# A hybrid encoder trunk: weight granules halved in the attention heads, and the first mixer reordered

## The reference

```
proj = rmsnorm(h, norm_mix) @ w_in[layer]
gate_b, gate_c, u, c_q, c_kv_full, gate_logits = split(proj)
y_a = (gate_b * shortconv(gate_c * u)) @ w_conv_out
# 16 heads, 64 + 32 (rotary) wide; queries and keys come from the latents c_q, c_kv
p = softmax(q k^T * scale + chunk mask);  y_b = (p v) @ w_o
g_a, g_b = sigmoid(gate_logits + b_gate)
h = h + (g_a * y_a + g_b * y_b) @ w_mix_out
```

## Time and profile before

| | before |
|---|---|
| time, median of 3 runs | 1182.83 us (1182.29 to 1185.14) |
| the profiled execution's own time | 1182.17 us |
| its span in the trace | 1180.4 us |
| TensorE busy | 1149.3 us (97%) |
| VectorE / ScalarE / GpSimd busy | 873.6 / 754.4 / 20.0 us |
| mean granted TensorE clock | 0.995 |

### The profile page before, as it was taken

How to read it: one execution, slowest core, us unless ns; L and a number is a source line. 1 busy time by engine, 2 the same in 40 slices (tenths; PEclk the granted TensorE clock), 3 DMA queues, 4 the chain that set the end, 5 groups by cost and what they waited for, 6 DMA issues and landing times.

```text
span 1180.4 us, 15901 instructions
## 1 busy us (share of the span) xinstructions
PE 1149.3 (97%) x5664; PEld 968.5 (82%) x5664; DVE 873.6 (74%) x987; ACT 754.4 (64%) x927; POOL 20.0 (2%) x59
## 2 busy tenths in 40 slices
PE   8999999999999999999999999999999999999986
PEld 7788788888888888887788888888888888888864
DVE  5557667666444546477666779999999999999993
ACT  6546565545444346456566456799878887888882
POOL 3000000000000001000000000000000000000000
PEclk9999999999999999999999999999999999999998
DMA  8755422659556354646333647999999999999991
GB/s 307 246 167 179 154 88 73 215 187 318 181 184 204 107 179 144 200 143 192 137 99 113 204 170 278 386 401 407 396 408 364 408 392 406 364 402 388 401 366 39
DMA packets 120555, 294.98 MB, mean 250 GB/s; under 512 B 9006, under 2 KB 33676, under 8 KB 119964
## 3 DMA queue, kind: packets, MB, share of 16 engines
q1 hardware_dynamic: 119376, 288.66, 67.9%
q0 software_dynamic: 960, 5.28, 1.2%
q10 hardware_dynamic: 140, 0.04, 0.0%
HBM read 292.90 MB, written 1.05 MB: 249 GB/s over the span
## 4 chain that ended last, share of the span: by engine, by line
PE 50%; issue 42%; ACT 4%; DVE 2%; DMA 1%; POOL 0%; SPq 0%; POOLq 0%; DVEq 0%; ACTq 0%
PE bank L1518 15%; PE bank L1519 15%; PE bank L1520 15%; PE bank L1556 2%; ACT w_hi L647 1%; DMA raw<-in_w_in 1%; PE bank L1719 1%; PE bank L1699 1%; ACT p_buf L775 1%; DVE mixed L1215 1%; PE bank L1707 1%; PE bank L1691 1%; DVE small L1218 1%; ACT pT L781 1%; PE bank L1755 0%
## 5 line engine op out<-in xcount | busy, mean ns | idle before, releaser
L1014 DVE TENSOR_TENSOR w_lo<-raw,w_hi 128x1536 fp32r<-128x1536 f32 (+3 forms) x144 | 242.9, 1693 | 178.2 <-ACT w_hi L647 177.7
L647 ACT ACTIVATE w_hi<-raw 128x1536 fp32r<-128x1536 f32 (+4 forms) x144 | 205.5, 1433 | 159.8 <-PE bank L1520 154.7
L1309 DVE TENSOR_TENSOR w_lo<-raw,w_hi 128x1792 fp32r<-128x1792 f32 (+3 forms) x148 | 287.4, 1968 | 15.1 <-ACT w_hi L830 14.8
L830 ACT ACTIVATE w_hi<-raw 128x1792 fp32r<-128x1792 f32 (+3 forms) x148 | 244.3, 1671 | 52.2 <-PE bank L1520 42.1
L1518 PE MATMUL bank<-w_hi,aT_hi 128*128 128x512 f32 (+1 forms) x592 | 235.8, 398 | 2.8 <-DVE w_lo L1014 2.8
L1520 PE MATMUL bank<-w_hi,aT_lo 128*128 128x512 f32 (+1 forms) x592 | 230.4, 389 | 0.0
L1519 PE MATMUL bank<-w_lo,aT_hi 128*128 128x512 f32 (+1 forms) x592 | 230.1, 389 | 0.0
L1518 PEld LDWEIGHTS bank<-w_hi,aT_hi 128*128 128x128 f32 x592 | 111.7, 189 | 25.0 <-issue 3.9
L1520 PEld LDWEIGHTS bank<-w_hi,aT_lo 128*128 128x128 f32 x592 | 111.4, 188 | 22.7
L1519 PEld LDWEIGHTS bank<-w_lo,aT_hi 128*128 128x128 f32 x592 | 111.7, 189 | 20.3
L1309 DVE TENSOR_TENSOR w_lo_more<-raw,w_hi_more 128x1792 fp32r<-128x1792 f32 (+3 forms) x50 | 96.9, 1944 | 6.8 <-ACT w_hi_more L830 6.8
(11 more groups left out here) (311 smaller groups left out, 1792.2 us busy)
## 6 DMA issues: line engine op xcount, KB each, us to landing
raw<-in_moe_w_gate SPq DMA_DIRECT2D x128, 448.0 KB, 6.7
raw<-in_moe_w_up SPq DMA_DIRECT2D x128, 448.0 KB, 6.3
raw<-in_moe_w_down SPq DMA_DIRECT2D x112, 512.0 KB, 6.7
raw<-in_w_in SPq DMA_DIRECT2D x40, 768.0 KB, 4.4
raw<-in_dense_w_gate SPq DMA_DIRECT2D x22, 512.0 KB, 4.0
raw<-in_dense_w_up SPq DMA_DIRECT2D x22, 512.0 KB, 4.8
raw<-in_dense_w_down SPq DMA_DIRECT2D x11, 1024.0 KB, 4.8
raw<-in_w_in SPq DMA_DIRECT2D x20, 512.0 KB, 4.7
```

What stands on the lines that cost most here:

```text
L647: act.activation(w_hi[:, weight_slot(b, j), 0:n], raw[:, b % 2, j, 0:n], ACT.Copy).then_inc(hi_made[j], 1)
L830: act.activation(split_of(hi_slot, m), raw_of(i, n), ACT.Copy).then_inc(e_hi_made, 1)
L1014: dve.tensor_tensor(w_lo[:, s, 0:n], raw[:, b % 2, j, 0:n], w_hi[:, s, 0:n].bitcast(F32), ALU.subtract).then_inc(lo_made[j], 1)
L1309: dve.tensor_tensor(split_of(lo_slot, m), raw_of(i, n), split_of(hi_slot, m).bitcast(F32), ALU.subtract).then_inc(e_lo_made, 1)
```

## The change

1. **Heads.** A new helper `hi_half` copies a granule in two halves (128x768, or 128x512 for j = 2). For the seven granules of steps 2 to 14, the first half comes at the end of step n and the second at the end of step n+1, and `lo` (still whole) moves to the end of step n+1. The granule of step 18 stays as it was. This holds in both layers.
2. **First mixer of layer 0.** ScalarE copies granule 0 of BLK_CU+1 before it waits for `lat_rstd`. The sines come behind the scaling of the latents, and granules 1 and 2 of BLK_CU+1 behind them. VectorE's `rotary_table` is cut in two: the part that needs the sines (`rotary_sines`) comes behind `lo` of BLK_CU's last granule and of BLK_CU+1's first.
3. **Table of functions.** The first activation of the program is a Sin instead of a Copy, so that the table that holds the sine is loaded at the start and not at L698.
4. **Gate bias.** The two transfers move from GpSimd's queue ahead of the latent roots to behind them, and wait for `out_made >= 3` (the first tile of BLK_CU+1 is multiplied).
5. A pad moves `ang`, `turns` and their neighbours to memory that `proj` doesn't use.

```
-            pool.dma_start(gates[:, 0, :], b_gate[0].partition_broadcast(P)).then_inc(bias_in, 16)
-            pool.dma_start(gates[:, 1, :], b_gate[0].partition_broadcast(P)).then_inc(bias_in, 16)
...
+                if L == 0:
+                    pool.wait_ge(out_made, 3)
+                    for t in range(NT):
+                        pool.dma_start(gates[:, t, :], b_gate[0].partition_broadcast(P)).then_inc(bias_in, 16)
...
+            def hi_half(b, j, n, first, part):
+
+                if part == 0:
+                    act.wait_ge(raw_in[j], raw_value(b, j, first))
+                    act.wait_ge(used[j], b)
+                cols_half = slice(part * n // 2, (part + 1) * n // 2)
+                half = act.activation(w_hi[:, weight_slot(b, j), cols_half], raw[:, b % 2, j, cols_half], ACT.Copy)
+                if part:
+                    half.then_inc(hi_made[j], 1)
...
-                    act.wait_ge(angle_made, 1)
-                    act.activation(ang[:, 2:4, :, :], ang[:, 0:2, :, :], ACT.Sin).then_inc(sines_made, 1)
...
+                if L == 0:
+                    hi(B + BLK_CU + 1, 0, SLAB_SIZES[0], B)
                 act.wait_ge(lat_rstd_made, 2 * (L + 1))
...
+                if L == 0:
+                    act.wait_ge(angle_made, 1)
+                    act.activation(ang[:, 2:4, :, :], ang[:, 0:2, :, :], ACT.Sin).then_inc(sines_made, 1)
                 for p in range(6):
-                    if p < 5:
+                    if L == 0 and p == 0:
+                        for j in (1, 2):
+                            hi(B + BLK_CU + 1, j, SLAB_SIZES[j], B)
+                    elif p < 5:
                         his(L, BLK_CU + p + 1)
...
-                    if n in GRANULE_AHEAD:
+                    for part in range(2):
+                        if n - part in GRANULE_AHEAD and n - part < HEADS + 2:
+                            b, j = GRANULE_AHEAD[n - part]
+                            hi_half(B + b, j, SLAB_SIZES[j], B, part)
+                    if n == HEADS + 2:
                         b, j = GRANULE_AHEAD[n]
                         hi(B + b, j, SLAB_SIZES[j], B)
...
-            act.activation(neg_max[:, 0:1], ident[:, 0:1], ACT.Copy)
+            act.activation(neg_max[:, 0:1], ident[:, 0:1], ACT.Sin)
...
                     lo(B + BLK_CU, 2, SLAB_SIZES[2])
+                    lo(B + BLK_CU + 1, 0, SLAB_SIZES[0])
+                    rotary_sines()
...
-                    if n in GRANULE_AHEAD:
-                        b, j = GRANULE_AHEAD[n]
+                    at = n if n == HEADS + 2 else n - 1
+                    if at in GRANULE_AHEAD:
+                        b, j = GRANULE_AHEAD[at]
                         lo(B + b, j, SLAB_SIZES[j])
```

More of the change, by code:

```diff
@@ L251, in build_trunk @@
             [("y1_hi", [P, D], F32R), ("y1_lo", [P, D], F32R)])
-        (proj, zT, q, k, v, sg_buf, hid_buf, hT_hi_buf, hT_lo_buf, rt, fold, sel, selT, slot_no, token_slot, chosen, tri, ones, tri_r, ones_r, counts, flag, iota_i, shift, key, key_base, top, order, rank_of, moved, slot_sorted, gate_sorted, slot_gate, ang, turns, rowc, row0, pos_i, posf, freq) = regions(
+        (proj, zT, q, k, v, sg_buf, hid_buf, hT_hi_buf, hT_lo_buf, rt, fold, sel, selT, slot_no, token_slot, chosen, tri, ones, tri_r, ones_r, counts, flag, iota_i, shift, key, key_base, top, order, rank_of, moved, slot_sorted, gate_sorted, slot_gate, _, ang, turns, rowc, row0, pos_i, posf, freq) = regions(
             [("proj", [P, 3, NT, D]), ("zT", [P, KC, S])],
@@ L265, in build_trunk @@
              ("gate_sorted", [P, NT, EXPERTS]), ("slot_gate", [P, 2, 2])],
-            [("ang", [P, 4, NT, RH]), ("turns", [P, 4, NT, RH]), ("rowc", [NCOL, P]), ("row0", [KC, P]),
+            [("early_pad", [P, 3, NT, D]), ("ang", [P, 4, NT, RH]), ("turns", [P, 4, NT, RH]), ("rowc", [NCOL, P]), ("row0", [KC, P]),
              ("pos_i", [P, NT], I32), ("posf", [P, NT]), ("freq", [P, RH])])
@@ L1075, in rotary_table, with rotary_sines @@
                 dve.tensor_scalar(ang[:, 1], ang[:, 0], 0.5, None, ALU.mult).then_inc(angle_made, 1)
+            def rotary_sines():
                 dve.wait_ge(sines_made, 1)
@@ L1141, in mixer @@
                 for p in range(6):
-                    if p < 5:
+                    if L == 0 and p == 0:
+                        for j in (1, 2):
+                            lo(B + BLK_CU + 1, j, SLAB_SIZES[j])
+                    elif p < 5:
                         los(L, BLK_CU + p + 1)
```

## The result

Device time, median of seven runs each: 1187.29 us after (1185.86 to 1188.24) against 1183.7 before (1182.29 to 1185.14; the 1182.83 of the table above is the median of three of them). The ratio is 1.0033 (95%: 1.0023 to 1.0043): the changed kernel is 3.6 us slower. The forecast was 1182.3, in a range that ended at 1187.0.

The account below looks back on a forecast made before the run. TensorE, working nearly all the time, was taken as the bound, so only its waits counted: -4.3 (first mixer) + 3.8 (heads, both layers) = -0.5 us, for a median of 1182.3 us; range 1178.5 to 1187.

Parts of the forecast that it names:

- Mixer, -4.3: First mixer, BLK_CU+1: TensorE's wait for `w_lo` (2.91 us) and the slow clock behind it (1.44) both go.
- the rival of a smaller gain: First mixer: a missing load halves the 4.3 us gain, giving 1184.5 us; chance 0.06.
- Bias transfers and table load at nothing: First mixer: moving the bias transfers and removing the 1.28 us table load were each counted as no gain or loss.
- Heads, +1.92 a layer: Heads: added waits in steps 5, 11 and 17 (4.25 us) less removed waits for `pT` (2.33), per layer.
- that alternative sum: Heads: with 0.3 us fixed per activation, a 768-column half takes 0.94, not 0.83; sum 0.7 us higher.
- the clock behind step 17: Heads, step 17: 2.07 us of waiting per layer was counted, with no slow clock behind it.
- The likeliest case: Whole kernel: the forecast as worked out, 1182.3 us, with no clock fall in step 17; chance 0.42.
- The clock falls in step 17: Rival, heads: TensorE's gap brings the 1.2 GHz level, 1.44 us in one or both layers: 1183.7 or 1185.2; chance 0.26.
- The rival with two falls: Heads, step 17: the clock falls in both layers, 1185.2 us; chance 0.26 for one or two falls.
- theory A: Heads: the low part, queued while its granule's second half is still being copied, holds VectorE's queue; next steps are late.

Follow-up runs that it names:

- e1: Kernel before with only the first-mixer edits, heads as before: 1179.46 us, ratio 0.9965, 4.2 us faster than before.
- e8: e1 with the two bias transfers back at their old place ahead of the latent roots: 1179.72 us, ratio 0.9970 against before.
- e4: Changed kernel plus 16 dummy transposes of the identity on TensorE in step 17: 1184.76 us, ratio 1.0011, 2.5 us faster than the changed kernel.
- e2: Kernel before with only the heads edits (halved granules, low part at the second half), mixer as before: 1190.13 us, ratio 1.0051, 6.5 us slower.
- e5: Kernel before with only the low parts moved one step later, granules copied whole in their old steps: 1179.46 us, ratio 0.9969, 3.8 us faster.
- e6: Changed kernel with whole granule copies in the old steps (mixer edits and moved low part together): 1175.26 us, ratio 0.9932 against before.
- e7: e6 plus a dummy one-column exponential behind ScalarE's first copy to `qkT` of a layer, loading the table early: 1174.32 us, ratio 0.9926 against before.
- e10: e1 with granule 0 of BLK_CU+1 copied behind the scaling instead of ahead of it: 1179.98 us, ratio 0.9974, 3.2 us faster than before.

## Why the prediction was wrong, point by point

- **Mixer, -4.3.** Right: 4.34 in the two traces, 4.2 in e1. Copy and low part of granule 0 stood where they were put (24.0 and 27.3 forecast, 24.07 and 27.37 found), and the clock stayed at 1.00. No load was missing, so the rival of a smaller gain fell. One step of the working was wrong without a price: the scaling was to start 2.1 earlier, at 25.8, and started at 27.61, as GpSimd was slower; granule 1 was copied at 28.99 and not at 27.4, still in time.
- **Bias transfers and table load at nothing.** Right for the bias (e8). For the table load nothing contradicts it: the mixer's 4.34 is the wait and its clock, with no room for another 1.28.
- **Heads, +1.92 a layer.** Right, place and size: 1.83 and 1.94 up to L1737 of step 17. Steps 5 and 11 lose 1.07 and 1.05 where 1.09 was forecast; L1737 of step 17 comes at +8.70 where +8.73 was; the waits at 4, 8, 12 and 14 are gone. The half of 768 columns takes 0.83 and the low part starts at S + 4.23, both as worked out. The Trainium skill, "ScalarE: Activation LUTs", What ACT_TABLE_LOAD costs, gives 186 ns + 0.833 ns per element for an activation with immediate scale and bias, 0.83 here; the trace agrees. The 0.3 us that the prediction took from its rules is meant for a bias held in memory, so that alternative sum was the wrong reading of the page.
- **The step that failed: the clock behind step 17.** The likeliest case had TensorE standing still 2.07 us there at no further price. The clock fell in both layers of the profiled execution, at 1.6 us each, which is the rival "The clock falls in step 17" in its upper form (priced 1.44 a layer, 1185.2, with a chance of 0.26 for one or two falls). e4 shows the cause: same place for L1737, no idle stretch, no fall, 2.5 us less. The prediction had the mixer's gap of 2.75 with its fall beside a forecast gap of 2.1 to 2.5, and no row of a gap of that size without one; the nearer row spoke for the fall, and I should have made it the likeliest. It would not have been certain: of the seven gaps of 2.4 to 2.8 us in the traces of before, after, e2 and e5, five were followed by a fall.
- **The last 2 us.** The rival with two falls said 1185.2, and 1187.29 was measured. Of the 2.1 us between them, 0.9 is no effect of the change: the sums started from a median of 1182.83 before, and over seven runs it is 1183.7. The rest is the change: with two falls the sum was -4.3 + 3.8 + 2.9 = +2.4, and +3.4 was found at 1151 us in the traces and 3.6 in the medians. Of the 1.0 between +2.4 and +3.4, 0.4 stands already ahead of the mixer (29.96 for 29.52), 0.4 is the price of the falls (1.6 for 1.44; TensorE had work in the whole slow stretch behind step 17, and none in the first half microsecond of the mixer's), and 0.4 arises between the heads of layer 1 and 1151 us, in code that both kernels have; the waits and the mixer came 0.1 to 0.2 cheaper than counted. Two falls at their stated price, counted from the 1183.7, make 1186.1: it took these small terms to carry the time past the range's end of 1187.0.
- **Why the heads lose at all.** The prediction's sentence for it, "`lo` is as long as before, and waits for a copy that comes a step later", is theory A, and it is right. But the sum was built per step, on which steps have one chunk, and so read as if steps 3, 9 and 15 were bad places. e5 puts the same low parts in the same steps and gains 3.8 us. The rows showed this: the earlier trace rows have the whole copy ending at 174.62 + 1.47 = S + 4.84, and VectorE free at 176.12 - 2.42 = S + 2.45, so a low part that is held until the next step finds its granule ready. The move was good, and the halving undid it.

## What to carry to other kernels

When work that needs another engine's result stands in an in-order queue, its producer must be done by the time the queue comes to it. Compare those two times in the trace before choosing the step: here the move of `lo` was worth 3.8 us, and with the copy split and the signal on its second half it cost 6.5 instead. And when a change puts an idle stretch of two or three us on TensorE, add the slow clock behind it to the likeliest sum if a gap of about that size in the same trace had one.

## What the runs showed of the hardware that was not expected

- **A gap of the same length brings the clock down in some executions and places and not in others.** A gap of 2.46 in step 17 was followed by 0.50 in both layers of the changed kernel, and in e2 a gap of that size in layer 0 was followed by 1.00 and in layer 1 by 0.50. In the first mixer a gap of 2.75 was followed by 0.50 before and one of 2.50 by 0.50 in e2, but in e5 one of 2.72 by 1.00, as its timeline and windows show:

```profile
32.46 0.47 PE L1519 MATMUL bank<-w_hi,aT_hi 128*128 128x512 f32 x1 [2.72 <-DVE w_lo L1014]
```

```profile
34.00:36.00 2.00, 2.00 (x11) 1.65 (x10) 1.12 (x1) 0.00 (x0) 0.00 (x0) 1.00 0.99 329
```

So a single trace says whether the clock fell in that execution, and not whether it always does; what decides it is not shown.

- **The slow stretch behind one and the same wait is not always as long.** Around the end of TensorE's wait of 4.3 to 4.7 us for `hid_buf` near the end, the clock was at 0.50 for about 3.4 us in the profile of before and in e6, and for about 6.8 us in those of the changed kernel, e1 to e5 and e7 to e10. What decides it was not found; the code there is the same in all of them. Of the 1.84 us by which the two spans differ beyond the 3.40, this is 0.66: the changed kernel is 3.40 behind at the end of that wait and 4.06 behind at TensorE's next (1168.93 before, 1172.99 after). The other 1.18 come later, where ScalarE stands still 1.71 us ahead of an activation that follows directly before, with nothing in the profile that it waited for. A window and that row, both of the changed kernel:

```profile
1156.00:1158.00 2.00, 2.00 (x6) 1.52 (x6) 1.59 (x2) 0.52 (x2) 0.00 (x0) 0.50 0.00 0
```

```profile
1177.23 0.60 ACT L1018 ACTIVATE hg<-bank 128x512 f32<-128x512 f32 x1 [1.71 <-issue]
```

- **The table load costs its own length and no more.** Timeline of ScalarE in the changed kernel, step 1:

```profile
132.11 0.60 ACT L785 ACTIVATE mixed<-bank 96x512 f32<-96x512 f32 x1 [1.94 <-PE bank L1729]
132.72 1.28 ACT L791 ACT_TABLE_LOAD   x1
134.02 0.40 ACT L791 ACTIVATE p_buf<-mixed,small 128x128 f32<-128x128 f32 x1
```

The next activation starts 1.30 us after the load does, and the one ahead of the load ended 0.02 us before it. The Trainium skill, "ScalarE: Activation LUTs", What ACT_TABLE_LOAD costs, puts a drain of about 1.4 us on top, 2.66 in all. The measurement decides: no drain shows on either side of the load.
